# A two-layer hybrid backbone on one core: the scan's two directions in step and without its own transposes, the retention's states formed beside its products, a narrower last input projection, and expert routing searched in halves

## What is computed

```python
for l in range(DEPTH):                      # DEPTH = 2
    need_ctx = l < DEPTH - 1                # the context is updated in layer 0 only
    z_x = modulate(rms_norm(x, g_norm1[l]), sh1, sc1) @ w_in[l]
    z_c = modulate(rms_norm(xc, g_norm1[l]), csh1, csc1) @ w_in[l]
    # columns of z: short conv (768) | latent attention (544) | RWKV (1024) | retention (1024)
    ...
    # RWKV, per head (4 heads of 64), forward and backward over the tokens:
    #   s = s*w - (s @ kk)(kk*a)' + v k' ;  y = s @ r
    # retention, per head and chunk of 128 tokens, forward and backward:
    #   r_state = r_state*gamma^128 + (k*zeta)' v ;  y = (q k' * dmat) v + (q*xi) r_state
    x = x + ga1 * (y_x @ w_out[l])
    # expert choice: 16 experts, each takes its top 128 of the 1024 latent tokens (32 of 256 context)
    aff = softmax(h @ w_router + b_router); gate, idx = top_k(aff.T, 2*n_tok//16)
    x = x + ga2 * experts(h[idx]) * gate, added back at idx
```

## Time and profile before

| | us |
|---|---|
| median of 3 runs | 4874.7 (4870.68 to 4875.51) |
| profiled execution, its own time | 4870.69 |
| its span, first to last instruction | 4868.8 |

### The profile page before, as it was taken

One profiled execution on the slowest core, in us unless ns is written; L12 is line 12 of the kernel. 1 busy time (PEld: TensorE's weight loads), 2 busy tenths in 40 slices (PEclk: granted clock), 3 DMA queues, 4 the chain that ended last, 5 costly groups with the idle time before them and its releaser, 6 DMA issues. The chain is left out here.

```text
span 4868.8 us, 64424 instructions
## 1 busy us (share of the span) xinstructions
PE 4017.1 (83%) x27764; PEld 2253.6 (46%) x27764; DVE 1579.1 (32%) x3277; ACT 793.1 (16%) x1792; POOL 450.7 (9%) x662
## 2 busy tenths in 40 slices
PE   6999688457779399999996999677466885899999
PEld 3645245445644144444443655344454742344444
DVE  2101454765633600000002101454666536100000
ACT  2000243133211000000002010243133210000000
POOL 0000100021200000001000000100021200000000
PEclk8999889688889599999997999789678987899999
DMA  4110400100045466677753110000100034688884
GB/s 151 62 72 11 138 34 10 50 20 16 3 176 222 171 229 229 243 264 259 262 186 84 59 71 16 26 3 22 45 12 16 3 126 181 240 312 309 311 327 161
DMA packets 196074, 624.94 MB, mean 128 GB/s; under 512 B 34473, under 2 KB 47017, under 8 KB 189137
## 3 DMA queue, kind: packets, MB, share of 16 engines
q1 hardware_dynamic: 173200, 548.13, 30.1%
q0 software_dynamic: 22592, 72.69, 4.9%
HBM read 566.90 MB, written 53.89 MB: 128 GB/s over the span
## 5 line engine op out<-in xcount | busy, mean ns | idle before, releaser
L484 PE MATMUL ps<-hT,p_w 128*128 128x512 f32 (+1 forms) x1344 | 486.2, 525 | 19.2 <-DMA p_w<-in_w_in_dram 19.2
L2177 PE MATMUL ps<-moe_w,e_xT 128*128 128x512 f32 x1024 | 451.2, 599 | 0.8 <-ACT e_xT L2239 0.8
L2214 PE MATMUL ps<-moe_w,e_hT 128*128 128x512 f32 x1024 | 445.9, 593 | 6.1 <-ACT e_hT L2258 6.1
L2184 PE MATMUL ps<-moe_w,e_xT 128*128 128x512 f32 x1024 | 444.7, 592 | 0.0
L487 PE MATMUL ps<-p_w,hT 128*128 128x272 f32 (+1 forms) x1280 | 422.3, 492 | 0.0
L484 PEld LDWEIGHTS ps<-hT,p_w 128*128 128x128 f32 x1344 | 258.1, 192 | 246.0 <-issue 213.3
L487 PEld LDWEIGHTS ps<-p_w,hT 128*128 128x128 f32 x1280 | 243.2, 190 | 178.9 <-issue 154.0
L2280 DVE TENSOR_TENSOR e_hid<-e_hid,ps 128x512 f32<-128x512 f32 x64 | 44.0, 688 | 838.6 <-PE ps L2184 838.6
L2177 PEld LDWEIGHTS ps<-moe_w,e_xT 128*128 128x128 f32 x1024 | 195.0, 192 | 247.2 <-issue 245.9
L2184 PEld LDWEIGHTS ps<-moe_w,e_xT 128*128 128x128 f32 x1024 | 194.6, 190 | 244.9 <-issue 244.9
L2214 PEld LDWEIGHTS ps<-moe_w,e_hT 128*128 128x128 f32 x1024 | 192.0, 190 | 239.0 <-issue 239.0
(11 more groups left out here) (328 smaller groups left out, 5555.1 us busy)
## 6 DMA issues: line engine op xcount, KB each, us to landing
moe_w<-in_w_gate_dram SPq DMA_DIRECT2D x64, 2048.0 KB, 13.3
moe_w<-in_w_up_dram SPq DMA_DIRECT2D x64, 2048.0 KB, 11.0
moe_w<-in_w_down_dram SPq DMA_DIRECT2D x64, 2048.0 KB, 16.9
o_mod_w<-in_w_ada_dram SPq DMA_DIRECT2D x24, 1024.0 KB, 11.1
p_w<-in_w_in_dram SPq DMA_DIRECT2D x10, 2048.0 KB, 8.0
m_mod_w<-in_w_ada_dram SPq DMA_DIRECT2D x16, 1024.0 KB, 6.6
z_rows<-p_zo POOLq DMA_DIRECT2D x40, 256.0 KB, 2.3
r_z<-z_rows SPq DMA_DIRECT2D x20, 512.0 KB, 3.3
```

What stands on the lines that cost most here:

```text
L484: ins = nc.tensor.matmul(ps[:, j % NB, 0:tw], w[:, n % RW, k, m * P:(m + 1) * P], hT[:, k, t0:t0 + tw], start=(k == 0), stop=(k == KT - 1))
L2177: ins = nc.tensor.matmul(ps[:, c, :], xT[:, 4 * half + k], wp[:, k, c * 512:(c + 1) * 512], start=(half == 0 and k == 0), stop=(half == 1 ...
L2184: ins = nc.tensor.matmul(ps[:, 2 + c, :], xT[:, 4 * half + k], wp[:, k, c * 512:(c + 1) * 512], start=(half == 0 and k == 0), stop=(half = ...
L2214: ins = nc.tensor.matmul(ps[:, 6 + c, :], hT2[:, 4 * half + k], wp[:, k, c * 512:(c + 1) * 512], start=(half == 0 and k == 0), stop=(half ...
```

## The change

In **project** of layer 1, jobs and columns of the context that nobody reads are left out: all nine 256-token jobs of the conv group and of RWKV tiles 0, 1 and 7; both context tiles of the first 272 columns, 112 columns of the second, half of each 512. POOL zeroes the unwritten conv part.

In **retention**, ACT copies V, POOL makes `kz` and multiplies gain into gate, PE forms only each head's own 64x64 block of the state sums (so no mask), DVE runs the forward recurrence tile by tile behind them, and loads are issued with the first rows ahead of the constants. POOL runs the backward recurrence in the second block, whose tiles now go in the backward order; ACT squares straight out of PSUM, and DVE multiplies out of PSUM.

In **rwkv_prep**, all token-row transposes are made by PE between the 15 rounds (70 of 128x128, in 20 units) and copied by ACT; the **scan** reads them. The scan's order has both directions at the same tile. In **topk**, `aff` holds the two halves of the latent tokens and the context on separate partitions, so 16 rounds over 512 elements do for all; then the two sorted lists are joined by a reversal matmul and six small DVE operations.

```diff
@@ stage_project
+    ctx_cols = {2: None, 3: (112, 272), 4: (256, 512), 5: (0, 256)}
+    ctx_tiles = range(2, 7)
...
-            jobs += [(n, t, None) for t in range(NT)]
+            jobs += [(n, t, None) for t in range(NT) if cols_of(n, t)]
...
-            jobs += [(n, m, s) for m in range(w // P) for s in range(3)]
+            jobs += [(n, m, s) for m in range(w // P) for s in range(3) if s or need_ctx or (kind == "rwkv" and o + m in ctx_tiles)]
...
+                    nc.gpsimd.memset(M[:, 0:6, 0:CTX], 0.0).then_inc(*pad.up())
@@ stage_retention, DVE of the first block
+                def scaled_queries(t):
...
+                    for d in range(2):
+                        nc.vector.tensor_tensor(QX[:, :, d, ts], QT[:, 0:2, ts], xi[:, :, d], ALU.mult)
+                def forward_state(t):
...
+                    for p in range(2):
+                        ins = nc.vector.scalar_tensor_tensor(SF[:, t + 1, p], SF[:, t, p], gd[:, p:p + 1],
+                                                             ps[:, 2 + t % 2, p * P:(p + 1) * P], ALU.mult, ALU.add)
...
+                for t in range(NT):
+                    if t + 1 < NT:
+                        rotated(t + 1)
+                    scaled_queries(t)
+                    if t >= 1:
+                        forward_state(t - 1)
@@ POOL of the first block, new
+                    for d in range(2):
+                        ins = nc.gpsimd.tensor_tensor(kz[:, t % 2, d], qk[:, t % 2, 4:8].rearrange("p h d -> p (h d)"), ze[:, d], ALU.mult)
+                    ins.then_inc(*kzd.up())
+                    pool.wait_ge(*gd_s.at(t + 1))
+                    nc.gpsimd.tensor_tensor(G[:, t], G[:, t], gr[:], ALU.mult).then_inc(*gg.up())
@@ POOL of the second block
+                    nc.gpsimd.tensor_tensor(new, old, gd[:].unsqueeze(2).broadcast_to([P, 2, P]), ALU.mult).then_inc(*decayed.up())
+                    pool.wait_ge(*decayed.at(n))
+                    nc.gpsimd.tensor_tensor(new, new, RB[:, back[n - 1]], ALU.add).then_inc(*sbd.up())
...
+                ahead = lead + 3
+                for n in range(ahead):
+                    state(n)
                 for n in range(N):
+                    if ahead + n < len(back):
+                        state(ahead + n)
                     pool.wait_ge(*g.vr.at(n + 1))
                     nc.gpsimd.tensor_tensor(s4[:, n % 2], s4[:, n % 2], g.mhalf[:, 0:H], ALU.pow).then_inc(*g.rq.up())
@@ stage_rwkv_prep, PE (in each of the 15 rounds) and ACT
+                for u in range(len(units) * n // (DB - 1), len(units) * (n + 1) // (DB - 1)):
+                    by_token(u)
...
+                nc.scalar.copy(BT[d][:, t].rearrange("p a n -> p (a n)"), ps[:, TBANKS[u % 4], 0:w]).then_inc(*tok_out.up())
@@ stage_rwkv_scan, PE
-                for now in slots():
...
+                for s in range(NT + 1):
+                    inv, car = s < NT, s > 0
+                    for d in DD:
+                        if car:
+                            w1_w2(d, s - 1)
+                    for d in DD:
+                        if inv:
+                            products(d, s)
+                        if car:
+                            carry_u(d, s - 1, 0)
+                    for d in DD:
+                        if inv:
+                            m_v(d, s)
+                        if car:
+                            carry_s(d, s - 1, 0)
+                        if inv:
+                            level_x(d, s, 0)
+                    for d in DD:
+                        if inv:
+                            level_t(d, s, 0)
+                        if car:
+                            carry_u(d, s - 1, 1)
...
@@ stage_topk, DVE
+                for r in range(CAPX // 8):
+                    v8 = val[:, 8 * r:8 * r + 8]
+                    link(nc.vector.max(v8, a))
+                    link(nc.vector.max_index(idx[:, 8 * r:8 * r + 8], v8, a))
+                    link(nc.vector.match_replace(a, v8, a, -1.0))
...
+                nc.vector.tensor_tensor(g.gate[:, 0], tt[:, 0, A], ps[:, 1, 0:NE], ALU.max)
```

More of the change, by code:

```diff
@@ L399, in stage_project, with cols_of @@
               (C_RWKV, 512, "rwkv", 0), (C_RWKV + 512, 512, "rwkv", 4)]
+    ctx_cols = {2: None, 3: (112, 272), 4: (256, 512), 5: (0, 256)}
+    ctx_tiles = range(2, 7)
+    def cols_of(n, t):
+        if t < NCT and not need_ctx:
+            return ctx_cols[n]
+        return 0, groups[n][1]
     jobs = []
@@ L554, in mix @@
                     zz = z[:, i % 2]
-                    last = rw0 + 3 * i + 2
+                    last = max(j for j in range(rw0, len(jobs)) if tile_of(j) == i)
                     for j in (last, last - 1):
@@ L1073, in _, with rotated @@
                 link = linker(dve, chain)
-                dve.wait_ge(*small.at(80))
-                for t in range(NT):
+                def rotated(t):
                     zz, q = z[:, t % 2], qk[:, t % 2]
@@ new lines, in _ @@
+                gate_values(0)
+                for t in range(NT):
+                    if t + 1 < NT:
+                        gate_values(t + 1)
+                    turned_out(t)
+                    if t >= 1:
+                        backward_sum(t - 1)
+                backward_sum(NT - 1)
+            @block.gpsimd
+            def _(pool):
+                pool.wait_ge(*small.at(80))
+                for t in range(NT):
+                    pool.wait_ge(*qkd.at(t + 1))
+                    if t >= 2:
+                        pool.wait_ge(*rm.at(t - 1))
+                    for d in range(2):
[3 more added lines that the diff above has]
+                    nc.gpsimd.tensor_tensor(G[:, t], G[:, t], gr[:], ALU.mult).then_inc(*gg.up())
@@ L1128, in _, with turned @@
             @block.tensor
             def _(pe):
-                for t in range(NT):
+                def turned(t):
                     pe.wait_ge(*qkd.at(t + 1))
@@ L1292, in stage_rwkv_prep, with sources @@
     allv, lnd, small = views(True), sg("ln_done"), sg("small_in")
+    turned, tok_out, ksd = sg("transposed"), sg("rw_tok"), sg("rw_ks")
+    BT, TBANKS = R["BYTOK"], (6, 3, 7, 4)
+    units = [(d, t) for t in range(NT) for d in range(2)]
+    def sources(d):
+        return (KR[d][:, 0], BK[d][:, 0], BK[d][:, 1]) + ((M[:, 4 + p],) if d == 0 else ())
     with nc.Block() as block:
@@ L1495, in toks, with rows @@
             return slice(order[d][s] * P + CH * c, order[d][s] * P + CH * c + CH)
+        def rows(d, s, a):
+            return BT[0 if a == 3 else d][:, order[d][s], a]
         with nc.Block() as block:
@@ L2019, in _ @@
             def _(sp):
+                sp.dma_start(flip[:], g.C["flip"]).then_inc(*small.up(16))
                 for j in range(MOE_RW):
```

447 lines of the change are left out of this document (250 added, 197 removed).

## The result

The changed kernel took 4569.1 us (median of four runs, 4558.5 to 4573.4) beside 4875.1 for the kernel before: a ratio of 0.937, 95% interval 0.935 to 0.939. The forecast was 4593, in a range of 4550 to 4643. The profiled execution has a span of 4571.2 us, 297.6 less than before.

The account below looks back on a forecast made before the run. PE bounds project, DVE bounds topk and retention's first block, and chains between engines bound retention's second block, rwkv_prep and scan. Terms -54 - 52 + 2 - 82 - 3 + 18 - 111 = -282 gave 4593 us, range 4550 to 4643.

Parts of the forecast that it names:

- the 2 us lost at the first gathers: Moe after topk: the shorter search ends before the weight load, so the first gather waits, 1 us lost per layer.
- I take 1.5: Retention's first block: DVE waits 1.5 us per tile for POOL's products, between 0 and 2.2, making 5.5 per tile.
- Rival (b): POOL and DVE hardly collide in retention and the scan step falls to 8.2 us: 4550 us, chance 0.12.
- the sign: Retention's first block: `ra` above its 0.68 us would show POOL and DVE colliding; staying at 0.68 would mean they hardly do.
- 0.73: Retention: assumed time in us of one POOL product of 256 elements, priced between 0.46 and 0.70 yet taken above.
- PE's groups need 2.75: Retention's second block: PE's matmul groups take 2.75 us per tile.
- I take 3.1: Retention's second block: a tile takes 3.1 us instead of about 3.5; layer 0 gains 3 us, layer 1 gains 0.
- rival (c): Scans: PE falls to the lower clock of 1.2 GHz, 2.2 us more per step: 4681 us, chance 0.05.
- the 0.13 us of a transpose: rwkv_prep: each of 70 added transposes costs PE 1.04/8 = 0.13 us, 9.1 us together.
- the 4.5 charged: rwkv_prep: added transposes and copies lengthen each of four preps by 4.5 us, 18 in all, bounds 4 and 36.
- The walk that gave 8.7 per step: Scan: following the new order through one step, each engine in its order, gave 8.7 us; 91.5 per scan, 111 gained in all.
- the outer bound that the prediction gave: Scan: the most favourable bound, 8.0 us per step, gaining 136 us over four scans.

Follow-up runs that it names:

- Experiment 10: Changed kernel with layer 1's project and both layers' topk put back as in the kernel before; 4664.8 us.
- experiment 4: Changed kernel with POOL's three products per tile of retention's first block (two kz, one gain) made by DVE instead; 4576.0 us.
- experiment 2: Changed kernel with two idle 512-column matmuls per tile of retention's first block from the third tile, PE also waiting for the constants; 4551.4 us.
- experiment 9: Changed kernel with two idle matmuls per first-block tile, two (layer 1: six) behind the second block's first scores, and 28 early rwkv_prep transposes; 4536.4 us, ratio 0.931 to before.
- experiment 12: The changed kernel itself measured once more, nothing altered; 4568.7 us, ratio 0.937 to the kernel before.
- experiment 1: Changed kernel with the whole retention stage of the kernel before; 4635.5 us.
- experiment 7: Changed kernel with two idle matmuls per first-block tile, plus four (layer 1: seven) behind the second block's first scores and one before each later group; 4552.3 us.
- Experiment 8: Changed kernel with 28 of rwkv_prep's 70 transposes made before its rounds; 4541.6 us.
- experiment 11: Kernel with joined idle matmuls and early transposes (4536 us), plus ten idle 512-column matmuls in each rwkv_prep before its diagonal blocks; 4541.2 us, ratio 0.932 to before.
- experiment 3: Changed kernel with four idle 512-column matmuls per tile of retention's first block; 4572.8 us.

## Why the prediction was right, and where it was not

**The total** was right in part by luck, because the two terms furthest off had opposite signs: 25 us more gain in the scans, 29 less in retention's second blocks. Without the second blocks' 29 us the kernel would have taken 4540, below the range. All others together gave 20 us more than forecast, 13 of it in the first blocks.

**Project, topk.** As priced: 59 for 54, 51 for 52. The windows hold 1324 - 1148 = 176 records fewer, the 144 + 32 of the sum; PE's busy time fell by 55.3. Experiment 10 shows the gains whole. For the 2 us lost at the first gathers, moe's two stages together took 1.1 us more, no more than they differ between the runs.

**Retention, first block.** 49.4 and 48.5 us for 56. The step at fault is "I take 1.5" for collisions: experiment 4 puts them near 1.0 per tile, none of them on the recurrence. Rival (b) had the direction right here, but POOL and DVE do collide: `rb` and `QX` went from 0.42 to 0.65 and 0.68 us, while `ra`, which the prediction named as the sign, went only to 0.75. POOL's products took 0.9 and 1.05 us, not 0.73 (a value above the 0.70 that the prediction had itself as the upper bound); they wait too.

**Retention, second block.** This is the step that failed. "PE's groups need 2.75" took PE's time at the full clock as given, and "I take 3.1" took each engine's work by itself. Two things stand in their place. At full clock a tile takes 3.98 us by the line through `on` that the profile after shows: 42.5 to 43.3 us on layer 0 (experiments 2 and 9) for the 38 forecast, some 4 us. On layer 1 experiment 9 took 38.8 for the 36 forecast, but its six idle matmuls held the first products back to 6.3 us into the block (3.4 in experiment 2); without them I estimate 36, as forecast. The rest, about 10 us on layer 0 and 11 to 14 on layer 1, is the clock. At 0.50 the same line takes 5.66 us a tile, and PE is busy 53.7 of 60.2 us (experiment 12). Before, the clock was up early (0.91 and 0.83 in the earlier trace rows, 0.92 and 0.90 in experiment 1). Experiments 2, 7 and 9 raise it by idle matmuls, and the block shortens; 2 and 7 change nothing else but the wait for the constants, and the early transposes of 9 come behind the block. I had weighed the clock for the scans only, as rival (c), and it did not come true there: 0.97.

**rwkv_prep.** +15 for +18. The last rounds came 0.9 us apart, not 1.13, but PE is the bound there, as forecast:

```profile
1000.00:1008.90 8.90, 8.90 (x80) 8.66 (x78) 7.81 (x39) 6.28 (x13) 0.00 (x0) 1.00 0.00 0
```

PE is busy without a gap, and DVE stands idle 1.1 of the 8.9 us. The term that was too large is the 0.13 us of a transpose, which spreads a group's last latency over its eight: here a record takes 8.90/80 = 0.11 us. Experiment 8 took 3.4 us per prep back, against the 4.5 charged.

**Scan.** 85.4 us for 91.5. The walk that gave 8.7 per step added each group's full latency, 0.45 us. In the new order PE's groups follow each other with little between, and 256 records took 8.1 us of busy time, or 32 ns each, which is the step. The gain of 136 us is the outer bound that the prediction gave, 8.0 per step. So the better estimate was there in the earlier trace rows: 98.64 us over 3200 records is 31 ns, times 256 is 7.9. The prediction used DVE's busy time as the floor and never PE's per record.

**What stays open.** Why the clock rises sooner in the old order is not settled: PE does the same 260 records there, and in the block before it was busy 28.2 of 96.7 us, less of the time than the 21.5 of 49.4 after the change; nor is why experiment 11 lost it on layer 0 where experiment 9 did not. I don't count stage_out's +6 us to the change: the same code, but for where it writes the affinities, took 205.3 to 211.4 us on layer 0 over the runs. Putting the normalisation of tile n-1 ahead of the variance of tile n on DVE should take the 1.00 us wait out of the second block, and releasing the bank after L1292 should, by the rows above, end it 0.46 us sooner, but only at full clock: at 0.50 there is 0.24 us to win. Neither was tried.

## What to carry to other kernels

Divide PE's busy time in a stage by its records and multiply by the records that will be left: if that is near the step you get by walking dependences, PE's throughput is the bound, and the walk is too long. Price a stage with short matmuls at both clocks, and look up the clock at which PE enters it: here a rearranged stage left PE at 0.50 where the old one, with PE busy a smaller share of the time, saw it rise early in the next block. And before an engine reads a PSUM bank that another used to copy out, look at what is queued ahead of that read, since the bank's next writer now waits for all of it.

## What the runs showed of the hardware

- The granted clock has two levels here, and instructions that do not change can meet either: one block of 260 records took 44.9 us in two profiles and 60.2 in two others. It stayed at 0.50 through the whole block with PE busy 53.7 of 60.2 us on layer 0 (experiment 12) and 42.9 of 50.1 us on layer 1. With two idle matmuls of 512 columns per tile in the block before (four in experiment 3) it rose within the first half of that block, on both layers, in all five kernels that had them.
- A clock once up was lost within 1.4 us of PE's return from a wait of 2.25 us (experiment 2, layer 1); it held on layer 1 in the three kernels that filled this wait (7, 9 and 11). In experiment 11 it was lost on layer 0 about 1 us behind a wait of 1.36 us, which experiment 9 had too and kept it.
- A POOL operation on 256 elements takes 0.72 us with DVE idle beside it (the state's sum in the second block), and the products of the first block 0.9 to 1.05 beside DVE; DVE's of two SBUF inputs goes from 0.42 to 0.68. Moving three such products from POOL to DVE lengthened the block by about 1 us.
- In the scan, whose matmuls are mostly 64x64, PE was busy 29 to 34 ns per record, in all four combinations of order and transposes.
